# A decoder layer on one core: the tokens of every matrix product are divided at 320 of 576 instead of at 288

## The chip, the core and the metric

The kernel runs on one core of a Trainium2 chip. The time is the device time of one execution in microseconds, the median of three runs. The engines of the core are TensorE (PE in the profile; its weight loads are PEld), VectorE (DVE), ScalarE (ACT), GpSimd (POOL) and SyncE (SP), which issues the loads of weights.

## The reference

One inference step of one layer of a hybrid decoder, in fp32, on 512 prompt positions and 8 x 8 sampled positions, 576 tokens in all, with a model width of 2048.

```python
h = rmsnorm(x, norm_mix_g[l])
p = h @ w_in                                   # 2048 -> 5120: u_A, v_A, B_gate, C_gate, x_B
u = gelu(p[..., :o1]); v = rmsnorm(gelu(p[..., o1:o2]), sgu_norm_g)
y_a = u * chunk_sgu(v, w_s, b_s)               # 8 heads, chunks of 128 positions
zc, new_mix = causal_dwconv(cg * xb, mix_prev, conv_mix_w, conv_mix_b)
y = concatenate([group_rmsnorm(y_a, ...), group_rmsnorm(bg * zc, ...)])
x = x + y @ w_out                              # 2048 -> 2048
h = rmsnorm(x, norm_ffn_g)
gate, new_ffn = causal_dwconv(h @ w_gate, ffn_prev, conv_ffn_w, conv_ffn_b)   # 2048 -> 5632
x = x + (silu(gate) * (h @ w_up)) @ w_down     # 5632 -> 2048
```

The outputs are the final RMSNorm of both token groups, the last rows of the convolution inputs, and the normalised `v` rows of the sampled tokens.

## The kernel before

Everything is held transposed: features on the 128 partitions, the 576 tokens along the free dimension. `h_hi`, `h_lo` and `X` are 16 rows (`KT`) of 576 columns, one after the other in SBUF, each row 2304 bytes of a partition. Their place starts at `h_at`, the first place of the arena, which is rounded up to 32 bytes.

Each product in fp32 precision is made of three matmuls of fp32r operands, in the helper `three` (L1159 to L1163): high part of the weights with the high part of the activations, high with low, low with high. Each matmul loads 128 x 128 weights and streams the columns of one part of the tokens.

The 576 tokens don't fit one PSUM bank of 512 fp32 columns, so each output tile of 128 features has a pair of banks: `pair(p, half)` (L155) gives bank 2p + half, columns 0 to `HALF`, with `HALF` = 288 (L43). `gemm` (L1165) goes through the left half of the tokens with all 16 rows, in two slots of weights of 8 rows each (48 matmuls), and then through the right half with the same weights (48 matmuls). Each slot is given back by `piece_done` when the right half is through with it. `gemm2_by_k` (L1183) makes the first two tiles of `w_out` and of the feed-forward part row by row, left and right in turn by three matmuls, because the rows of its input are just being made. `down_tile` (L1365) adds a block of two rows of the activation (`act_hi`, `act_lo`) into one output tile of the down projection: six left matmuls, then six right.

The weights come as pieces of 128 x 1024: SyncE loads one into `raw` (two buffers), ScalarE rounds it to `w_hi` (`split_hi`, L485), VectorE makes `w_lo` from the rest (`split_lo`, L769). There are four slots of `w_hi` and `w_lo`. A product needs two, so while it runs on two, the other two are refilled; in the feed-forward loop (`ffn_block`, L1382) the sequence is gate tile, 16 down tiles of the block before, up tile, gate tile, up tile.

VectorE empties the banks: `times_rb` (L778) multiplies by the reciprocal norm, `w_out_tile` (L1021) and `down_add` (L1086) add to `X`, `gate_in` (L1058) writes the padded input of the convolution and so splits the right half into the rest of the prompt (224 columns) and the 64 sampled tokens. In each of them the left bank is read by one instruction and the right by the next, behind one wait for the whole tile. PSUM banks 4 to 7 serve small sums, transposes and the head mixing between the products; in the feed-forward loop they are two more pairs.

At the start, x comes in five blocks of tokens (four of 128, one of 64) and is transposed on TensorE. The first product may begin its left half when three blocks, 384 columns, are ready; `rest_of_x` (L1226) waits for the others before its right half.

Of the kernel before, what the change touches and what calls it, by code (L numbers as in the profile page):

```python
# [23 lines left out]
ALU = mybir.AluOpType  # L24
# [3 lines left out]
P = 128  # L28


def build_layer(nc, x_prompt, x_sample, state_conv_mix, state_conv_ffn, norm_mix_g, w_in, sgu_norm_g,
# [4 lines left out]
    _, SEQ, DM = x_prompt.shape  # L36
# [3 lines left out]
    assert w_s.shape[2] == P and AW % P == 0 and conv_mix_b.shape[1] == AW and DM == 2 * AW  # L40
    SAMP = NB * NS
    T = SEQ + SAMP
    HALF = T // 2  # L43
    KT = DM // P
    HEADS = AW // P
    TB = SEQ // P
# [12 lines left out]
    with ctx:  # L59
        def psum(name, shape):  # L60
            return ctx.enter_context(nc.psum_tensor(name, shape, F32))

        def sem(name):
            return ctx.enter_context(nc.semaphore(name))
# [7 lines left out]
        def sb(name, shape, dt=F32, at=None):  # L72
            n = 4
            for s in shape[1:]:
                n *= s
            n = -(-n // 32) * 32
            off = place[0] if at is None else at
            if at is None:
                place[0] += n
                assert place[0] <= base + ARENA, (name, place[0] - base)  # L80
            return nc.alloc_sbuf_tensor_at(name, shape, dt, offset=off)
# [4 lines left out]
        X = sb("X", [P, KT, T])  # L86
# [36 lines left out]
        rb = sb("rb", [P, T])  # L123
        zpad = sb("zpad", [P, ZP])
# [28 lines left out]
        ps = psum("ps", [P, 8, 512])  # L153

        def pair(p, half):  # L155
            return ps[:, 2 * p + half, 0:HALF]

        T_BANK, SSQ_BANK, MIX_BANK = 4, 5, 6
        t_samp = ps[0:SAMP, 7, 0:128]
# [9 lines left out]
        down_added = sem("down_added")  # L169
# [21 lines left out]
        tile_read = sem("tile_read")  # L191
# [51 lines left out]
        zs = zpad[:, 2 + SEQ:ZP].rearrange("p (b t) -> p b t", b=NB)  # L243

        def samp8(ap):

            return ap.rearrange("p (b t) -> p b t", b=NB)
# [13 lines left out]
        def blk_q(b):  # L261

            return b * 12 + (GEMM_PIECES - 4)

        def blk_p(b):

            return b * 8 + GEMM_PIECES
# [494 lines left out]
        def _(dve):  # L762

            v = nc.vector

            def row(buf, k):
                return buf[:, ds(k, 1), :].rearrange("p a t -> p (a t)")
# [9 lines left out]

            def times_rb(dst, p, done):  # L778

                v.tensor_tensor(dst[:, 0:HALF], pair(p, 0), rb[:, 0:HALF], ALU.mult)  # L780
                v.tensor_tensor(dst[:, HALF:T], pair(p, 1), rb[:, HALF:T], ALU.mult).then_inc(done, 1)  # L781

            def reciprocal_rms(n, dst):
                dve.wait_ge(rms_ready, n)
# [15 lines left out]
            for tb in range(TB + 1):  # L800
                n = P if tb < TB else SAMP
# [21 lines left out]
            for tb in range(TB + 1):  # L823
                n = P if tb < TB else SAMP
# [98 lines left out]
            with dve.Fori(1, HEADS // 2 - 1) as i:  # L923
                for s in range(2):
                    n = i * 2 + (s + 1)
# [95 lines left out]
            def w_out_tile(m, s, done=None):  # L1021

                dve.wait_ge(piece_done, m * 2 + (IN_PIECES + 2) if done is None else done)
                xm = row(X, m)
                v.tensor_tensor(xm[:, 0:HALF], xm[:, 0:HALF], pair(s, 0), ALU.add)
                v.tensor_tensor(xm[:, HALF:T], xm[:, HALF:T], pair(s, 1), ALU.add).then_inc(tile_read, 1)


            split_lo(IN_PIECES + 4, 0)
# [28 lines left out]
            def gate_in(f, p, done):  # L1058

                dve.wait_ge(piece_done, done)  # L1060
                dve.wait_ge(rows_saved, f + HEADS)
                n = SEQ - HALF
                v.tensor_tensor(zpad[:, 2:2 + HALF], pair(p, 0), rb[:, 0:HALF], ALU.mult)  # L1063
                v.tensor_tensor(zpad[:, 2 + HALF:2 + SEQ], ps[:, 2 * p + 1, 0:n], rb[:, HALF:SEQ], ALU.mult)
                v.tensor_tensor(zs[:, :, 2:], samp8(ps[:, 2 * p + 1, n:HALF]), samp8(rb[:, SEQ:T]),  # L1065
                                ALU.mult).then_inc(z_ready, 1)

            def gate_conv(f):
# [16 lines left out]

            def down_add(j, p, done):  # L1086
                dve.wait_ge(down_done, done)
                v.tensor_tensor(X[:, j, 0:HALF], X[:, j, 0:HALF], pair(p, 0), ALU.add)  # L1088
                v.tensor_tensor(X[:, j, HALF:T], X[:, j, HALF:T], pair(p, 1), ALU.add).then_inc(down_added, 1)  # L1089

            g0 = GEMM_PIECES
            split_lo(g0 + 4, 0)
            gate_in(0, 0, g0 + 3)
            split_lo(g0 + 5, 1)
            gate_conv(0)
# [7 lines left out]
            with dve.Fori(1, NBLK) as b:  # L1103
                q, p, d = blk_q(b), blk_p(b), (b - 1) * 16
# [44 lines left out]
            for tb in (0, 2, 4):  # L1149
                n = P if tb < TB else SAMP  # L1150
# [5 lines left out]
        def _(pe):  # L1156
# [8 lines left out]
            def gemm(q, c, p, q1=None, mid=None, q3=None):  # L1165


                for half in range(2):
                    cols = slice(half * HALF, (half + 1) * HALF)
                    for s in range(2):  # L1170
                        if half == 0:
                            pe.wait_ge(lo_ready, q + s + 1)
                        for k in range(PK):
                            kk = s * PK + k
                            last = three(pair(p, half), w_hi[:, (c + s) % 4, k, :], w_lo[:, (c + s) % 4, k, :],
                                         h_hi[:, kk, cols], h_lo[:, kk, cols], kk == 0, kk == KT - 1)
                        if half == 1:
                            last.then_inc(piece_done, 1)
                        hook = (q1, mid, q3, None)[2 * half + s]
                        if hook is not None:  # L1180
                            hook()

            def gemm2_by_k(q, ready, after):  # L1183


                for kk in range(KT):
                    s, k = kk // PK, kk % PK
                    pe.wait_ge(ready, kk + 1)
                    for tile in range(2):
                        c = 2 * tile + s  # L1190
                        if k == 0:
                            pe.wait_ge(lo_ready, q + c + 1)
                        for half in range(2):
                            cols = slice(half * HALF, (half + 1) * HALF)
                            last = three(pair(tile, half), w_hi[:, c, k, :], w_lo[:, c, k, :],
                                         h_hi[:, kk, cols], h_lo[:, kk, cols], kk == 0, kk == KT - 1)
                        if k == PK - 1:
                            last.then_inc(piece_done, 1)
                    if kk in after:
                        after[kk]()  # L1200
# [10 lines left out]
            for tb in range(TB + 1):  # L1211
                n = P if tb < TB else SAMP
# [39 lines left out]
                          start=True, stop=True).then_inc(corner_done, 1)  # L1252


            assert HALF <= 3 * P
            pe.wait_ge(xlo_pool, 2 * 3)
            pe.wait_ge(xlo_dve, 2 * 3)
            gemm(0, 0, 0, mid=rest_of_x)
# [106 lines left out]
            def down_tile(slot, jj, p, ks=(0, 1)):  # L1365

                for half in range(2):
                    cols = slice(half * HALF, (half + 1) * HALF)
                    for k in ks:
                        last = three(pair(p, half), w_hi[:, slot, 4 * k + jj, :], w_lo[:, slot, 4 * k + jj, :],  # L1370
                                     act_hi[:, k, cols], act_lo[:, k, cols], k == 0, k == 1)
                if ks[-1] == 1:
                    last.then_inc(down_done, 1)
# [88 lines left out]
            for tb in range(TB + 1):  # L1462
                n = P if tb < TB else SAMP
# [29 lines left out]
```

## Time and profile before

| | |
|---|---|
| median of 3 runs | 2510.88 us (2510.07 to 2511.1) |
| span of the profiled execution | 2507.9 us |
| mean granted clock of TensorE | 0.992 |
| matmuls in the span | 18473 |
| of these 128 x 128 by 288 columns | 18048 |
| loaded from memory | 208 MB, 87 GB/s with what is written |

The profile is of one execution. Its page gives busy times of each engine, the chain of work that ended last (followed back from the last instruction), and groups of instructions by line. The durations of matmuls on it overlap, since matmuls are pipelined and their ends are modelled; how often one starts after another is read from the timeline. The granted clock of TensorE is 1.0 (2.4 GHz) from about 60 us to the end of the products; before that it changes between the two levels.

### The profile page before, as it was taken

To read this page: it belongs to the slowest core of one execution; us is meant where nothing else is said; L and a number is where in the kernel's file an instruction comes from. 1 tells how busy PE (TensorE), PEld (TensorE's weight loads), DVE (VectorE), ACT (ScalarE), POOL (GpSimd) and SP (SyncE) were. 2 spreads that over 40 slices of the span, in tenths; PEclk is the share of its full clock that TensorE was granted. 3 is DMA by queue.
4 is the path that set the end of the run, shared out by engine and by line. 5 is a ranking of instruction groups with operands and counts; after the bars stand their busy time and mean duration, and the time that the engine had idled before them with its cause. 6 is when DMAs were issued, how large, how long until landed. Compare 5 with 4: busy or idle time off the path is not lost.

```text
span 2507.9 us, 45612 instructions
## 1 busy us (share of the span) xinstructions
PE 2462.1 (98%) x18473; PEld 2452.1 (98%) x18473; DVE 1206.8 (48%) x1902; ACT 617.1 (25%) x738; POOL 160.2 (6%) x279
## 2 busy tenths in 40 slices
PE   6999999999999999999999999999999999999996
PEld 6999999999999999999999999999999999999996
DVE  6357644556224535455434444444544354454445
ACT  6224312113113322222212222122222211222224
POOL 3310000001221000000000000000000000000004
PEclk8999999999999999999999999999999999999998
DMA  5422222224222222223222222222232222222222
GB/s 153 159 84 71 69 85 85 83 85 151 83 79 73 84 80 81 84 84 92 75 84 84 84 84 81 80 80 82 78 97 78 76 84 84 84 84 84 84 85 84
DMA packets 326837, 219.17 MB, mean 87 GB/s; under 512 B 6804, under 2 KB 301839, under 8 KB 324992
## 3 DMA queue, kind: packets, MB, share of 16 engines
q1 hardware_dynamic: 324432, 203.98, 27.2%
q0 software_dynamic: 2352, 14.41, 1.6%
q8 instruction: 41, 0.67, 0.1%
q14 instruction: 12, 0.10, 0.0%
HBM read 208.19 MB, written 10.18 MB: 87 GB/s over the span
## 4 chain that ended last, share of the span: by engine, by line
PE 96%; ACT 1%; DVE 1%; POOL 0%; issue 0%; DMA 0%; POOLq 0%; SPq 0%; DVEq 0%; ACTq 0%
PE ps L1161 32%; PE ps L1163 31%; PE ps L1162 31%; DVE h_lo L797 0%; POOL acc L470 0%; ACT ps L540 0%; PE ps L1284 0%; ACT h_hi L512 0%; PE ps L1297 0%; DMA x_nat<-in_x_prompt_dram 0%; ACT X L520 0%; PE ps L1296 0%; ACT w_hi L491 0%; DVE rms L813 0%; PE ps L1276 0%
## 5 line engine op out<-in xcount | busy, mean ns | idle before, releaser
L1161 PE MATMUL ps<-h_hi,w_hi 128*128 128x288 f32 x4608 | 1362.2, 296 | 6.2 <-issue 4.9
L1163 PE MATMUL ps<-h_hi,w_lo 128*128 128x288 f32 x4608 | 1358.7, 295 | 0.0
L1162 PE MATMUL ps<-h_lo,w_hi 128*128 128x288 f32 x4608 | 1358.3, 295 | 0.0
L1161 PEld LDWEIGHTS ps<-h_hi,w_hi 128*128 128x128 f32 x4608 | 865.6, 188 | 8.4 <-issue 5.8
L1162 PEld LDWEIGHTS ps<-h_lo,w_hi 128*128 128x128 f32 x4608 | 865.7, 188 | 0.0
L1163 PEld LDWEIGHTS ps<-h_hi,w_lo 128*128 128x128 f32 x4608 | 865.7, 188 | 0.0
L771 DVE TENSOR_TENSOR w_lo<-raw,w_hi 128x1024 fp32r<-128x1024 f32 x376 | 460.5, 1248 | 305.7 <-ACT w_hi L491 305.6
L491 ACT ACTIVATE w_hi<-raw 128x1024 fp32r<-128x1024 f32 x376 | 384.2, 1050 | 489.9 <-PE ps L1163 474.5
L1161 PE MATMUL ps<-act_hi,w_hi 128*128 128x288 f32 x1408 | 418.4, 297 | 1.0 <-DVE scaled L781 1.0
L1163 PE MATMUL ps<-act_hi,w_lo 128*128 128x288 f32 x1408 | 415.0, 295 | 0.0
L1162 PE MATMUL ps<-act_lo,w_hi 128*128 128x288 f32 x1408 | 414.3, 294 | 0.0
L1161 PEld LDWEIGHTS ps<-act_hi,w_hi 128*128 128x128 f32 x1408 | 264.4, 188 | 1.2 <-issue 1.2
L1163 PEld LDWEIGHTS ps<-act_hi,w_lo 128*128 128x128 f32 x1408 | 264.2, 188 | 0.0
L1162 PEld LDWEIGHTS ps<-act_lo,w_hi 128*128 128x128 f32 x1408 | 264.0, 187 | 0.0
L780 DVE TENSOR_TENSOR scaled<-ps,rb 128x288 f32<-128x288 f32 x68 | 31.1, 457 | 443.6 <-PE ps L1163 431.2
L1088 DVE TENSOR_TENSOR X<-X,ps 128x288 f32<-128x288 f32 x352 | 158.3, 450 | 81.4 <-PE ps L1163 81.4
L1063 DVE TENSOR_TENSOR zpad<-ps,rb 128x288 f32<-128x288 f32 x44 | 20.2, 458 | 305.8 <-PE ps L1163 305.8
L1089 DVE TENSOR_TENSOR X<-X,ps 128x288 f32<-128x288 f32 x352 | 157.3, 447 | 0.0
L620 ACT ACTIVATE cv<-zpad,ffnv 128x592 f32<-128x592 f32 x44 | 38.8, 882 | 417.8 <-DVE zpad L1065 417.8
L697 ACT ACTIVATE act_hi<-prod 128x576 fp32r<-128x576 f32 x44 | 30.2, 686 | 429.1 <-DVE prod L1080 429.1
L429 POOL COPY ffn_rows<-zpad 128x2 f32 x44 | 8.2, 187 | 1310.6 <-DVE zpad L1065 1310.6
L693 ACT ACTIVATE gate_act<-cv 128x592 f32<-128x592 f32 x44 | 30.8, 700 | 200.1 <-DVE cv L954 200.1
(184 smaller groups left out, 921.6 us busy)
## 6 DMA issues: line engine op xcount, KB each, us to landing
raw<-in_w_gate_dram SPq DMA_DIRECT2D x88, 512.0 KB, 3.9
raw<-in_w_up_dram SPq DMA_DIRECT2D x88, 512.0 KB, 3.8
raw<-in_w_down_dram SPq DMA_DIRECT2D x88, 512.0 KB, 4.3
raw<-in_w_in_dram SPq DMA_DIRECT2D x80, 512.0 KB, 4.3
raw<-in_w_out_dram SPq DMA_DIRECT2D x32, 512.0 KB, 4.0
xT_scratch<-X POOLq DMA_DIRECT2D x1, 4608.0 KB, 18.5
X<-xT_scratch POOLq DMA_DIRECT2D x4, 1152.0 KB, 5.6
x_nat<-in_x_prompt_dram SPq DMA_DIRECT2D x4, 1024.0 KB, 8.6
```

Of the source, the lines that this page charges most:

```text
L491: a.activation(w_hi[:, c % 4], raw[:, c % 2], ACT.Copy).then_inc(hi_ready, 1)
L620: a.activation(cv[:, :], zpad[:, 2:ZP], ACT.Identity, bias=b, scale=w).then_inc(tap2_done, 1)
L693: a.activation(gate_act[:, :], cv[:, :], ACT.Silu).then_inc(silu_done, 1)
L697: a.activation(act_hi[:, s, :], prod[:, :], ACT.Copy).then_inc(acthi_ready, 1)
L771: v.tensor_tensor(w_lo[:, c % 4], raw[:, c % 2], w_hi[:, c % 4].bitcast(F32), ALU.subtract).then_inc(lo_ready, 1)
L780: v.tensor_tensor(dst[:, 0:HALF], pair(p, 0), rb[:, 0:HALF], ALU.mult)
L1063: v.tensor_tensor(zpad[:, 2:2 + HALF], pair(p, 0), rb[:, 0:HALF], ALU.mult)
L1088: v.tensor_tensor(X[:, j, 0:HALF], X[:, j, 0:HALF], pair(p, 0), ALU.add)
L1089: v.tensor_tensor(X[:, j, HALF:T], X[:, j, HALF:T], pair(p, 1), ALU.add).then_inc(down_added, 1)
L1161: te.matmul(out, whi, xhi, start=start, stop=False)
L1162: te.matmul(out, whi, xlo, start=False, stop=False)
L1163: return te.matmul(out, wlo, xhi, start=False, stop=stop)
```

## The change

The left part of the tokens becomes five ninths, 320 columns, the right part 256. The two bounds stand in `CUTS`, and each place that used `HALF` uses them: the PSUM view `pair`, the columns that `gemm`, `gemm2_by_k` and `down_tile` stream, and VectorE's reads of the banks. The number of matmuls, weight loads, semaphores and waits is the same, and so is their order. In `gate_in` the right part's piece of the prompt is 192 columns instead of 224.

```diff
-    HALF = T // 2
+    LEFT = 5 * (T // 9)
+    CUTS = (0, LEFT, T)
...
         def pair(p, half):
-            return ps[:, 2 * p + half, 0:HALF]
+            return ps[:, 2 * p + half, 0:CUTS[half + 1] - CUTS[half]]
...
             def times_rb(dst, p, done):
 
-                v.tensor_tensor(dst[:, 0:HALF], pair(p, 0), rb[:, 0:HALF], ALU.mult)
-                v.tensor_tensor(dst[:, HALF:T], pair(p, 1), rb[:, HALF:T], ALU.mult).then_inc(done, 1)
+                v.tensor_tensor(dst[:, 0:LEFT], pair(p, 0), rb[:, 0:LEFT], ALU.mult)
+                v.tensor_tensor(dst[:, LEFT:T], pair(p, 1), rb[:, LEFT:T], ALU.mult).then_inc(done, 1)
...
-                n = SEQ - HALF
-                v.tensor_tensor(zpad[:, 2:2 + HALF], pair(p, 0), rb[:, 0:HALF], ALU.mult)
-                v.tensor_tensor(zpad[:, 2 + HALF:2 + SEQ], ps[:, 2 * p + 1, 0:n], rb[:, HALF:SEQ], ALU.mult)
-                v.tensor_tensor(zs[:, :, 2:], samp8(ps[:, 2 * p + 1, n:HALF]), samp8(rb[:, SEQ:T]),
+                n = SEQ - LEFT
+                v.tensor_tensor(zpad[:, 2:2 + LEFT], pair(p, 0), rb[:, 0:LEFT], ALU.mult)
+                v.tensor_tensor(zpad[:, 2 + LEFT:2 + SEQ], ps[:, 2 * p + 1, 0:n], rb[:, LEFT:SEQ], ALU.mult)
+                v.tensor_tensor(zs[:, :, 2:], samp8(ps[:, 2 * p + 1, n:T - LEFT]), samp8(rb[:, SEQ:T]),
                                 ALU.mult).then_inc(z_ready, 1)
...
-                v.tensor_tensor(X[:, j, 0:HALF], X[:, j, 0:HALF], pair(p, 0), ALU.add)
-                v.tensor_tensor(X[:, j, HALF:T], X[:, j, HALF:T], pair(p, 1), ALU.add).then_inc(down_added, 1)
+                v.tensor_tensor(X[:, j, 0:LEFT], X[:, j, 0:LEFT], pair(p, 0), ALU.add)
+                v.tensor_tensor(X[:, j, LEFT:T], X[:, j, LEFT:T], pair(p, 1), ALU.add).then_inc(down_added, 1)
...
                 for half in range(2):
-                    cols = slice(half * HALF, (half + 1) * HALF)
+                    cols = slice(CUTS[half], CUTS[half + 1])
```

The last edit is made in `gemm`, `gemm2_by_k` and `down_tile`, and the pair of adds also in `w_out_tile`.

## Rows read from the trace of the kernel before

**Rows 1.** Busy time of the engines over the span, from the page
```profile
PE 2462.1 (98%) x18473; PEld 2452.1 (98%) x18473; DVE 1206.8 (48%) x1902; ACT 617.1 (25%) x738; POOL 160.2 (6%) x279
```

**Rows 2.** Chain that ended last, shares of the span by engine and line
```profile
PE 96%; ACT 1%; DVE 1%; POOL 0%; issue 0%; DMA 0%; POOLq 0%; SPq 0%; DVEq 0%; ACTq 0%
PE ps L1161 32%; PE ps L1163 31%; PE ps L1162 31%; DVE h_lo L797 0%; POOL acc L470 0%; ACT ps L540 0%; PE ps L1284 0%; ACT h_hi L512 0%; PE ps L1297 0%; DMA x_nat<-in_x_prompt_dram 0%; ACT X L520 0%; PE ps L1296 0%; ACT w_hi L491 0%; DVE rms L813 0%; PE ps L1276 0%
```

**Rows 3.** TensorE's waits: us in total, times, longest; three of nine rows
```profile
PE ps L1219 <- ACT X L520: 7.7, 6, 3.3
...
PE ps L1161 <- issue: 4.9, 2, 2.9
...
PE ps L1161 <- DVE X L1026: 0.3, 1, 0.3
```

**Rows 4.** Groups of instructions: count | busy us, mean ns | idle before
```profile
L1161 PE MATMUL ps<-h_hi,w_hi 128*128 128x288 f32 x4608 | 1362.2, 296 | 6.2 <-issue 4.9
...
L1161 PE MATMUL ps<-act_hi,w_hi 128*128 128x288 f32 x1408 | 418.4, 297 | 1.0 <-DVE scaled L781 1.0
...
L1088 DVE TENSOR_TENSOR X<-X,ps 128x288 f32<-128x288 f32 x352 | 158.3, 450 | 81.4 <-PE ps L1163 81.4
```

**Rows 5.** A stretch: us, busy of PE, PEld, DVE, ACT, POOL; PEclk, DMA, GB/s
```profile
1000.00:1100.00 100.00, 100.00 (x756) 100.00 (x755) 50.02 (x89) 23.17 (x27) 1.62 (x9) 1.00 0.28 84
```

**Rows 6.** TensorE's timeline (start, duration): first left, first right, next tile
```profile
1048.49 0.29 PE L1161 MATMUL ps<-h_hi,w_hi 128*128 128x288 f32 x1
...
1054.81 0.30 PE L1161 MATMUL ps<-h_hi,w_hi 128*128 128x288 f32 x1
...
1061.21 0.29 PE L1161 MATMUL ps<-h_hi,w_hi 128*128 128x288 f32 x1
```

**Rows 7.** The same timeline, one down tile: first left, first right, next tile
```profile
1010.28 0.29 PE L1161 MATMUL ps<-act_hi,w_hi 128*128 128x288 f32 x1
...
1011.07 0.30 PE L1161 MATMUL ps<-act_hi,w_hi 128*128 128x288 f32 x1
...
1011.87 0.29 PE L1161 MATMUL ps<-act_hi,w_hi 128*128 128x288 f32 x1
```

**Rows 8.** TensorE's timeline, sums of 512 and 64 columns between products
```profile
179.32 0.40 PE L1296 MATMUL ps<-sq_hi,ones_r 128*128 128x512 f32 x1
...
179.79 0.19 PE L1296 MATMUL ps<-sq_hi,ones_r 128*128 128x64 f32 x1
179.82 0.27 PE L1297 MATMUL ps<-sq_lo,ones_r 128*128 128x64 f32 x1
179.93 0.38 PE L1161 MATMUL ps<-h_hi,w_hi 128*128 128x288 f32 x1
180.15 0.30 PE L1162 MATMUL ps<-h_lo,w_hi 128*128 128x288 f32 x1
```

**Rows 9.** TensorE's timeline in the first product, granted clock 0.50
```profile
38.32 0.44 PE L1162 MATMUL ps<-h_lo,w_hi 128*128 128x288 f32 x1
38.56 0.44 PE L1163 MATMUL ps<-h_hi,w_lo 128*128 128x288 f32 x1
```

**Rows 10.** TensorE's timeline, second slot of the products after `gemm2_by_k`
```profile
610.70 0.39 PE L1161 MATMUL ps<-h_hi,w_hi 128*128 128x288 f32 x1 [0.27 <-DVE X L1026]
...
822.00 0.29 PE L1163 MATMUL ps<-h_hi,w_lo 128*128 128x288 f32 x1
822.43 0.40 PE L1161 MATMUL ps<-h_hi,w_hi 128*128 128x288 f32 x1
```

**Rows 11.** Groups of instructions, as in rows 4: the splitting of the weights
```profile
L771 DVE TENSOR_TENSOR w_lo<-raw,w_hi 128x1024 fp32r<-128x1024 f32 x376 | 460.5, 1248 | 305.7 <-ACT w_hi L491 305.6
L491 ACT ACTIVATE w_hi<-raw 128x1024 fp32r<-128x1024 f32 x376 | 384.2, 1050 | 489.9 <-PE ps L1163 474.5
```

**Rows 12.** TensorE's timeline, four transposes and what follows them
```profile
160.90 0.60 PE L1276 MATMUL ps<-ident,vn 128*128 128x128 f32 x4
161.34 0.27 PE L1277 MATMUL ps<-ident,vn 128*64 128x128 f32 x1
```

More of the change, by code:

```diff
@@ L1024, in w_out_tile @@
                 xm = row(X, m)
-                v.tensor_tensor(xm[:, 0:HALF], xm[:, 0:HALF], pair(s, 0), ALU.add)
-                v.tensor_tensor(xm[:, HALF:T], xm[:, HALF:T], pair(s, 1), ALU.add).then_inc(tile_read, 1)
+                v.tensor_tensor(xm[:, 0:LEFT], xm[:, 0:LEFT], pair(s, 0), ALU.add)
+                v.tensor_tensor(xm[:, LEFT:T], xm[:, LEFT:T], pair(s, 1), ALU.add).then_inc(tile_read, 1)
             split_lo(IN_PIECES + 4, 0)
@@ L1193, in gemm2_by_k @@
                         for half in range(2):
-                            cols = slice(half * HALF, (half + 1) * HALF)
+                            cols = slice(CUTS[half], CUTS[half + 1])
                             last = three(pair(tile, half), w_hi[:, c, k, :], w_lo[:, c, k, :],
@@ L1252, in corner @@
                           start=True, stop=True).then_inc(corner_done, 1)
-            assert HALF <= 3 * P
+            assert LEFT <= 3 * P
             pe.wait_ge(xlo_pool, 2 * 3)
@@ L1367, in down_tile @@
                 for half in range(2):
-                    cols = slice(half * HALF, (half + 1) * HALF)
+                    cols = slice(CUTS[half], CUTS[half + 1])
                     for k in ks:
```

## The prediction

> **What bounds the kernel now.** I read the page's busy table first: TensorE is busy 98% of the span in matmuls and weight loads alike, VectorE 48%, ScalarE 25% [rows 1]. A busy TensorE could still be an engine waiting inside modelled durations, so I went to the chain that ended last: 96% of it is TensorE, and three lines of the helper `three` carry 94% [rows 2]. The third view is the list of what TensorE waited for: nine rows, from 7.7 down to 0.3 us, 27 us in all, nearly all of it ahead of the first product and between stages [rows 3]. So the time is a count times a period: 3 x 4608 products on `h` and 3 x 1408 on `act`, 18048 in all, each 288 columns wide [rows 4]. The mean duration printed there (295 ns) overlaps its neighbours and is no period. The period comes from the stretches: 756 matmuls in 100 us at full clock, 132.3 ns each [rows 5]. 18048 x 132.5 = 2391 us of the 2507.9 us span; the rest is the start, the end, the transposes and small sums. What matters is therefore the period at 320 and at 256 columns, and nothing else by much: 1 ns on the mean of the two is 18 us, 0.7% of the time. The measurement of this kernel can tell about 0.2%, that is 5 us or 0.28 ns per matmul.
>
> **What the trace says of the period.** In one undisturbed product of a tile, the 48 matmuls of the left half go from 1048.49 to 1054.81 (6.32 us, 131.7 ns each) and the 48 of the right half from there to 1061.21 (6.40 us, 133.3 ns each) [rows 6]. The down products show the same order: six left ones 0.79 us, six right ones 0.80 us [rows 7]. So the two halves of equal width differ by 1.6 ns, and I don't know the cause. The one other width of the same operand type is 512: two matmuls of 512 columns follow each other and the next starts 0.47 us after the first, 235 ns each (the 16 such pairs lie within 4 ns of that) [rows 8]. The line through (288, 132.5) and (512, 235) has a slope of 102.5 / 224 = 0.458 ns per column and passes zero columns at +0.7 ns: time is proportional to columns, 2.18 columns per ns, with hardly a fixed part. At 1.2 GHz the same 288 columns take 0.24 us, 1.2 columns per ns and no more [rows 9].
>
> **The change part by part.**
> (1) The 9024 left matmuls grow from 288 to 320 columns: +32 x 0.458 = +14.7 ns, 147.2 ns. The 9024 right ones shrink to 256: -14.7 ns, 117.8 ns. Sum per pair: 265.0 ns as before, so +132.3 us and -132.3 us, net 0. This holds for every straight line, with or without a fixed part; no matmul, weight load, semaphore or wait is added. Only a departure from the line inside 256 to 320 counts, and the trace has no row there. I bound it from both sides below, under the rivals, and take 0 because both measured widths lie on a line through nearly nothing.
> (2) A wait: `gemm` starts its second slot of weights 24 left matmuls after the first. After each of the two products by rows (`gemm2_by_k`), the slot was freed late and the matmul that needs it starts late: with 0.27 us of idle time before it at 610.70, and 0.43 us after its predecessor at 822.43, where 0.13 us is the rule, so 0.30 us late [rows 10]. The 24 left matmuls ahead of it now last 24 x 14.7 = 0.35 us longer, while the slot's refill (one ScalarE copy, one VectorE subtraction) begins at the same moment. Both waits, 0.27 and 0.30 us, are covered by that: -0.6 us. What is late next is nothing: the right half behind is shorter by the same 0.35 us.
> (3) Slots in the steady part are given back after the first half of the right pass, which now ends 9.88 us instead of 9.52 us into a product of 12.7 us: 0.35 us later. ScalarE and then VectorE refill it from `raw`, in 1.05 and 1.25 us [rows 11]; the slot is wanted a whole product later, 12.7 us. The cost is nothing; if that cover were gone it would be at most 0.35 us a tile, for which a wait of every tile on VectorE's `w_lo` would have to stand in the wait list, and none does [rows 3].
> (4) VectorE reads both banks after the right part is done. The add to `X` of one bank takes 450 ns [rows 4]. If all of that were by the column, 1.6 ns each, the left read grows by 0.05 us and the right shrinks by as much; the prompt's piece in `gate_in` goes from 224 to 192 and the left grows by the same 32. Sum 0, and it lies beside TensorE, except at the ends of stages, where the sum is equal too.
> (5) The first product starts at 1.2 GHz [rows 9], and the clock rises within its left half. The left half waits for three blocks of x, as before, since 320 columns are still within 384; the wait for the rest of x shows no idle time, and comes later now. 0 us.
> (6) At the end, `down_tile` of the last block is paced partly by GpSimd's sums. They start from the VectorE add, whose sum is equal. 0 us.
> Sum: 2507.9 - 0.6 = 2507.3 us for the profiled execution. The median of the runs is 2510.9, 3.0 us above the span; so 2510.3.
>
> At one place a rule of the Trainium skill bears on this. The page "TensorE: Matmul & The Clock Gate", section "Back-to-back issue gap", gives N / 2.4 + 2.5 ns: an estimate from it is 122.5 ns for 288 columns, where this trace has 132.5; so its slope (0.417) is too small here. By its formula 135.8 and 109.2 ns would have the same mean as two of 122.5, so the sum would still be 0.
>
> **The rivals.**
> (A) The period depends on where the read starts. Rows of `h_hi` are 576 x 4 = 2304 bytes, nine times 256. The cut at 288 puts the right half 1152 bytes in, 4.5 times 256; at 320 it is 1280, five times 256, in step with the left half. If the 1.6 ns by which right exceeds left [rows 6, 7] comes from that half step, the right part becomes as cheap as the left: 9024 x 1.6 = 14.4 us less, 2495.8 us. For: the difference is there in two kinds of product, with equal width, equal weights and the same rows. Against: left and right also go to different banks of PSUM, and that doesn't change; and the left read could as well be the odd one.
> (B), the slower side: the read goes in blocks of 256 bytes, and each block touched costs something. Today both halves lie in step at one end and half a block off at the other, five blocks each. Whether the buffer itself starts on a block can't be seen. If it is half a block off, 320 columns touch six and 256 touch five: eleven for ten. The price: 288 columns at 2.4 GHz are 120 ns, so 12.5 ns of the 132.5 are over; divided by five blocks, 2.5 ns each. One more block for each pair is 9024 x 2.5 = +22.6 us, 2532.8 us. It decides only if the buffer starts off a block. If it starts on one, the blocks would be 5 + 4, nine for ten, and the same price would be a gain to 2487.6. Against both: 512 columns are 21.7 ns over their 213.3, which a straight line explains as well.
> (C) The weight load becomes the bound of the right part. Each matmul loads 128 columns of weights, and in one stretch the trace shows that this has a price: after two matmuls of 64 columns (179.79) the starts are 0.03, 0.11 and 0.22 us apart, 0.36 us for three, although the streams would be 0.03, 0.03 and 0.13 [rows 8]. Taken as three loads in a row that is at most 120 ns a load, against 117.8 ns for a right matmul; taken with the last one as a 288-column stream of 132 ns, it is 114 ns. The transposes of 128 columns, each with its load, are 0.44 us for four, 110 ns [rows 12]. So the floor is 110 to 120 ns: below the 117.8 it costs nothing, at 120 it costs 2.2 x 9024 = 19.9 us, 2530.1. The transposes are the plainest row of a load per matmul; I take no cost, and keep the other end.
> The Trainium skill's same page, section "LDWEIGHTS (loading the stationary operand)", gives columns / 1.2 ns; an estimate from it is 106.7 ns for this load, under the 117.8, and the transposes' 110 ns agrees with it.
> (D) The change doesn't do what it says: the program would have to split differently from the text. The shapes are static, so I give this nothing.
>
> **How the numbers follow.** Straight line, within 5 us of 2510.3: 0.42. Start of the read (A) and blocks from an aligned buffer, 2488 to 2500: 0.28. Blocks from an unaligned buffer (B), 2525 to 2535: 0.18. Weight load or the like (C), 2516 to 2530: 0.12. Predicted is the straight line's 2510.3; its own range is 2505 to 2515. The range over the cases reaches down to A with a little over, 2494, and up past B's price, 2534; it leaves out the block gain and larger losses, together under 0.2. Faster by over 0.2%: 0.28; within 0.2%: 0.42; slower by over 0.2%: 0.30.
>
> **What the profile after would show.** (1) right and the line holding: 48 left matmuls of a product in 7.07 us, 48 right in 5.65 us, and again 756 in 100 us. If A: the left at 146.3 ns or so and the right at 117 ns, both on one line. If B: both above the line by one block's 2.5 ns in part. If C: the left on the line and the right above 118 ns, whatever the left does. (2) right: the gaps at the two places near 0.13 us. (3) and (4): the wait list as short as before. The prediction is wrong if the sum of one left and one right period departs from 265 ns by more than 0.6 ns; the other terms together can't move 1 us.

## The result, and the profile after

The changed kernel takes 2524.1 us (2522.4 to 2525.3) where the kernel before took 2511.0 in the same comparison: 1.0049 times as long, with an interval of 1.0034 to 1.0063. The forecast of no change was wrong: it is 0.5% slower, by about 13 us, inside the stated range but clear of zero. The profiled span went from 2507.9 to 2521.4 us.

The page's busy table, in the columns of [rows 1], and the chain, in those of [rows 2]:

```profile
PE 2475.4 (98%) x18473; PEld 2465.8 (98%) x18473; DVE 1206.4 (48%) x1902; ACT 617.1 (24%) x738; POOL 160.5 (6%) x279
PE 96%; ACT 1%; DVE 1%; POOL 0%; issue 0%; DMA 0%; POOLq 0%; SPq 0%; DVEq 0%; ACTq 0%
```

The same picture and the same counts: TensorE alone carries the end, VectorE did the same work in the same time. TensorE's waits show nothing new either (us in total, times, longest; the first three of nine rows, for [rows 3]; lines after L43 are one further on in this kernel):

```profile
PE ps L1220 <- ACT X L521: 7.9, 6, 3.5
PE ps L1220 <- DMA x_nat<-in_x_prompt_dram: 6.3, 2, 3.3
PE ps L1162 <- issue: 4.9, 2, 2.9
```

So the time came from the period. TensorE's timeline (start, duration) in the feed-forward part shows the first right matmul of a tile, the first left one of the next, its first right one and the first left one after it; the last three answer to [rows 6]:

```profile
1048.32 0.28 PE L1162 MATMUL ps<-h_hi,w_hi 128*128 128x256 f32 x1
...
1054.08 0.31 PE L1162 MATMUL ps<-h_hi,w_hi 128*128 128x320 f32 x1
...
1061.12 0.28 PE L1162 MATMUL ps<-h_hi,w_hi 128*128 128x256 f32 x1
...
1066.88 0.31 PE L1162 MATMUL ps<-h_hi,w_hi 128*128 128x320 f32 x1
```

48 left matmuls take 7.04 us, 146.7 ns each; 48 right ones 5.76 us, 120.0 ns each. The pair is 266.7 ns; it was 131.7 + 133.3 = 265.0 ns. Over all tiles, by the median tile: in the 13440 matmuls of `gemm` the period rose from 132.5 to 133.3 ns, 0.81 ns each, 10.9 us; in the 4224 of the down products from 132.75 to 133.33, 2.5 us; in the 384 of `gemm2_by_k` it was 133.3 and stayed. That is 13.4 us of the 13.5 by which the span grew.

From here on it helps to count in array cycles at 2.4 GHz, 0.4167 ns each, and to take the width off: the left half before took 316 cycles (288 + 28), the right 320 (288 + 32); after the change they take 352 (320 + 32) and 288 (256 + 32). The widths add to 576 in every case. What moved is the surcharge, the cycles above the width: 60 a pair became 64, and the four are all the left half's, 28 before and 32 after; the right half pays 32 at either width.

### The profile page after: what moved, and what is told of

It reads as the page before. It is cut to its first block, busy times and chain, and to the rows that moved or that the text cites. A ratio compares the mean times of both kernels' runs of the same rounds, so it can differ in the third digit from the quotient of the medians.

```text
span 2521.4 us, 45612 instructions
## 1 busy us (share of the span) xinstructions
PE 2475.4 (98%) x18473; PEld 2465.8 (98%) x18473; DVE 1206.4 (48%) x1902; ACT 617.1 (24%) x738; POOL 160.5 (6%) x279
## 4 chain that ended last, share of the span: by engine, by line
PE 96%; ACT 1%; DVE 1%; POOL 0%; issue 0%; DMA 0%; POOLq 0%; SPq 0%; DVEq 0%; ACTq 0%
PE ps L1162 32%; PE ps L1164 31%; PE ps L1163 31%; DVE h_lo L798 0%; POOL acc L471 0%; ACT ps L541 0%; PE ps L1285 0%; ACT h_hi L513 0%; PE ps L1298 0%; ACT X L521 0%; DMA x_nat<-in_x_prompt_dram 0%; PE ps L1297 0%; PE ps L1277 0%; DVE rms L814 0%; PE ps L1446 0%
## 5 line engine op out<-in xcount | busy, mean ns | idle before, releaser
L1162 PE MATMUL ps<-h_hi,w_hi 128*128 128x256 f32 (+1 forms) x4608 | 1369.5, 297 | 6.0 <-issue 4.9
L1163 PE MATMUL ps<-h_lo,w_hi 128*128 128x256 f32 (+1 forms) x4608 | 1365.6, 296 | 0.0
L1164 PE MATMUL ps<-h_hi,w_lo 128*128 128x256 f32 (+1 forms) x4608 | 1365.5, 296 | 0.0
L1162 PE MATMUL ps<-act_hi,w_hi 128*128 128x256 f32 (+1 forms) x1408 | 418.0, 297 | 1.0 <-DVE scaled L782 1.0
L1164 PE MATMUL ps<-act_hi,w_lo 128*128 128x256 f32 (+1 forms) x1408 | 416.7, 296 | 0.0
L1163 PE MATMUL ps<-act_lo,w_hi 128*128 128x256 f32 (+1 forms) x1408 | 416.7, 296 | 0.0
L781 DVE TENSOR_TENSOR scaled<-ps,rb 128x320 f32<-128x320 f32 x68 | 33.3, 490 | 445.9 <-PE ps L1164 433.4
L1089 DVE TENSOR_TENSOR X<-X,ps 128x320 f32<-128x320 f32 x352 | 169.6, 482 | 83.9 <-PE ps L1164 83.9
L1064 DVE TENSOR_TENSOR zpad<-ps,rb 128x320 f32<-128x320 f32 x44 | 21.7, 492 | 310.3 <-PE ps L1164 310.3
L1090 DVE TENSOR_TENSOR X<-X,ps 128x256 f32<-128x256 f32 x352 | 145.1, 412 | 0.0
```

The costliest lines, as they stand in the source:

```text
L781: v.tensor_tensor(dst[:, 0:LEFT], pair(p, 0), rb[:, 0:LEFT], ALU.mult)
L1064: v.tensor_tensor(zpad[:, 2:2 + LEFT], pair(p, 0), rb[:, 0:LEFT], ALU.mult)
L1089: v.tensor_tensor(X[:, j, 0:LEFT], X[:, j, 0:LEFT], pair(p, 0), ALU.add)
L1090: v.tensor_tensor(X[:, j, LEFT:T], X[:, j, LEFT:T], pair(p, 1), ALU.add).then_inc(down_added, 1)
L1162: te.matmul(out, whi, xhi, start=start, stop=False)
L1163: te.matmul(out, whi, xlo, start=False, stop=False)
```

## The experiments

The kernels that are timed differ from the changed kernel, or in one case from the kernel before, by the one to three lines shown. Each stream kernel is the kernel before with matmuls behind its last one whose results nothing reads; its time as a whole means nothing. A stream is a row of 32 to 96 equal matmuls, and the granted clock is 1.0 in all streams quoted but those of 96 to 160 columns in the last section.

### Widths on their own, three theories

```diff
             last.then_inc(fssq_done, 1)
+            mv = act_hi[:, :, :].rearrange("p k t -> p (k t)")
+            def probe(i, n, a, bank, m=P, src=mv, same=False):
+                return (ps[0:m, bank, 0:n], w_hi[:, 0, 0 if same else i % PK, 0:m], src[:, a:a + n])
+            for i in range(64): te.matmul(*probe(i, 256, 0, 2), start=i == 0, stop=i == 63)
...
```

> The kernel before, and behind its last matmul 57 short streams of fp32r matmuls (64 or 96 each, 128 columns of weights, eight weight blocks in turn) that nothing reads: widths 64 to 512 from the first column of act_hi, then 288 columns from eleven other starts, two banks, weights of 64 and 32 columns, one weight block again and again, and high, low, high in turn. In the changed kernel 320 columns take 146.7 ns and 256 take 120.0 ns, that is each width plus 32 array cycles of 2.4 GHz. Theory 1, a fixed cost of 32 cycles a matmul, which only 288 columns in the left half escape: 256 columns 120.0 ns, 272 columns 126.7, 304 columns 140.0, 240 columns 113.3, each 16 columns 6.7 ns. Theory 2, a floor near 120 ns from the weight load (rival C) over a line of 0.458 ns per column: 224, 240 and 256 columns all about 120 ns, 272 columns about 125 and 304 about 140; 64 weight columns lower the floor, so that 256 columns then take about 117.8 ns or less. Theory 3, the start of the read (rivals A and B): 288 columns change with the start in steps of 64 or 256 bytes, by 1.6 ns or more, and 256 columns take less at one of the starts 0, 32, 64 and 320 than at the others.

The view is that of one source line: count, duration (min/median/max), first and last start in us, shape. The period is the distance of the two starts by 63:

```profile
L1481 PE MATMUL ps<-act_hi,w_hi x64: 269/274/280, 2578.5 to 2585.5; 128*128 128x240 f32 x64
L1483 PE MATMUL ps<-act_hi,w_hi x64: 278/283/283, 2592.9 to 2600.4; 128*128 128x256 f32 x64
L1485 PE MATMUL ps<-act_hi,w_hi x64: 284/288/291, 2608.2 to 2616.1; 128*128 128x272 f32 x64
L1487 PE MATMUL ps<-act_hi,w_hi x64: 290/295/298, 2624.4 to 2632.7; 128*128 128x288 f32 x64
L1489 PE MATMUL ps<-act_hi,w_hi x64: 296/301/303, 2641.5 to 2650.2; 128*128 128x304 f32 x64
L1491 PE MATMUL ps<-act_hi,w_hi x64: 308/309/313, 2659.5 to 2668.7; 128*128 128x320 f32 x64
L1501 PE MATMUL ps<-act_hi,w_hi x64: 294/294/297, 2770.7 to 2779.1; 128*128 128x288 f32 x64
L1512 PE MATMUL ps<-act_hi,w_hi x64: 274/281/287, 2864.0 to 2871.4; 128*128 128x256 f32 x64
L1521 PE MATMUL ps<-act_hi,w_hi x64: 274/276/280, 2936.0 to 2943.1; 128*64 128x256 f32 x64
```

From the single starts, which are kept in ns, the means past the first few are:

| columns (from column 0) | 208 to 240 | 248 | 256 | 264 | 272 | 280 | 288 | 296 | 304 | 312 | 320 | 352 | 384 | 448 | 512 |
|---|---|---|---|---|---|---|---|---|---|---|---|---|---|---|---|
| ns | 111.6 | 113.3 | 120.0 | 120.0 | 125.4 | 127.9 | 131.8 | 136.0 | 137.7 | 142.7 | 146.7 | 160.0 | 173.3 | 206.7 | 227.1 |
| cycles above the width | (floor) | 24 | 32 | 24 | 29 | 27 | 28 | 30 | 27 | 31 | 32 | 32 | 32 | 48 | 33 |

The streams give the periods of the kernels to 0.1 ns (131.7 for the old left, 146.7 and 120.0 for the new halves), although no other engine and no DMA works beside them. Neither contention nor the schedule has a part in it. From 248 to 384 columns the surcharge is no line: it goes up and down between 24 and 32 cycles, and beyond them it has 48 at 448 columns and 33 at 512. 288 columns from column 32 (L1501) take 133.3 ns, as from column 288, where the old right half began; from 0, 64, 128, 192 and 256 they take 131.7, and from 144 as well. The bank makes no difference (131.8 in bank 3). Nor does the turn of `act_hi` and `act_lo`, or one weight block again and again (131.6 each). Theory 1 falls with 264 and 304 columns. Theory 2 falls with 224 and 240, which were to take about 120 ns as 256 do: a floor exists, and it lies at 111.6 ns, where 208, 224 and 240 columns are alike, 8 ns under what 256 columns take. Weights have a part all the same: with 64 weight columns (L1521) the same 256 columns take 113.5 ns, 16 cycles above the width instead of 32. But 320 columns stay at 146.7 with them, and 512 take 230.0, more than the 227.1 with 128. Theory 3 is right for 288 columns, and for 256 too: they are at +32 from 0, 64 and 320, but take 118.6 ns from 32 (L1512). Only 320 columns don't depend on the start here, at +32 from 0, 32, 64 and 256.

### The change mirrored

```diff
-    LEFT = 5 * (T // 9)
+    LEFT = 4 * (T // 9)
```

> The changed kernel mirrored: left part 256 columns, right part 320. Theory 1 (fixed cost by width) and theory 2 (floor under 256 columns): left 120.0 ns, right 146.7 ns, the time as after the change, 2524 us, but for the two waits for a slot of weights behind the products by rows, which grow by 0.35 us each. Theory 3 (the start of the read or the bank of the left half is what was cheap at 288 columns): the time differs from 2524 us by more than 3 us.

2524.9 us (2523.8 to 2526.5), 1.0050 with an interval of 1.0033 to 1.0067. The periods changed sides, as theories 1 and 2 had it: 120.0 left, 146.7 right. Side and bank have no part in the loss.

### Half of the change

```diff
-    LEFT = 5 * (T // 9)
+    LEFT = 304
```

> Half of the change: the cut at 304, a left part of 304 columns and a right part of 272. Theory 1 (width plus 32 cycles for every width but the equal halves): 140.0 and 126.7 ns, 133.3 in the mean, the time as after the change, 2523 us. Theory 2 (a floor near 120 ns that 272 columns stay above, on a line of 0.458 ns per column): 139.7 and 125.2 ns, 132.5 in the mean, the time as before, 2510 us. Theory 3: right part starts 1216 bytes in, 4.75 times 256, so it is as dear as at 288 or dearer, 2511 us or more.

2480.6 us (2477.7 to 2481.5), 0.9874 with an interval of 0.9858 to 0.9891: 1.3% faster than before, which no theory had. TensorE's timeline, first left, first right, next tile:

```profile
1050.73 0.30 PE L1162 MATMUL ps<-h_hi,w_hi 128*128 128x304 f32 x1
...
1057.34 0.29 PE L1162 MATMUL ps<-h_hi,w_hi 128*128 128x272 f32 x1
...
1063.26 0.30 PE L1162 MATMUL ps<-h_hi,w_hi 128*128 128x304 f32 x1
```

6.61 us and 5.92 us, 137.7 and 123.3 ns: surcharges of 27 and 24 cycles, 51 a pair instead of 60. 272 columns from column 0 had 125.4 ns as a stream, from column 304 they have 123.3. So going half the way gains and going the whole way loses; a slope between two widths cannot say what a third one costs.

### Every buffer 128 bytes further on

```diff
-        place = [base]
+        place = [base + 128]
```

> The kernel before with 288 and 288 columns, every buffer in SBUF 128 bytes further on, the distances between them as they were. Theory 3 (where the read starts against blocks of 256 bytes decides, rivals A and B): left and right change roles, 133.3 ns for the left and 131.7 for the right. Theories 1 and 2: nothing changes, 131.7 and 133.3 ns, and the time stays at 2511 us.

2511.8 us, 1.0002 with an interval of 0.9993 to 1.0012, and 131.6 to 131.7 left and 133.4 right in the products, as before. Left and right did not change roles, so the start of the read against fixed places of 256 bytes (rival A as it stood) is out. Rival B is not tested by this: 1152 bytes touch five blocks by its count whether the buffer is shifted or not. What matters for 288 columns is not where they lie in SBUF but where they lie against something that moved with them.

### All cuts, and starts and weights moved

```diff
+            def probe(i, n, a, off=0, m=P):
+                return (ps[0:m, 2, 0:n], wv[:, off + (i % PK) * P:off + (i % PK) * P + m], mv[:, a:a + n])
...
+            for i in range(48): te.matmul(*probe(i, 256, 0, 16), start=i == 0, stop=i == 47)
...
```

> The kernel before, and behind its last matmul 111 streams of 48 fp32r matmuls that nothing reads: for 34 cuts c from 248 to 328 the left part (c columns from column 0) and the right part (576 - c columns from column c); then 256, 320, 304 and 272 columns from starts 8 to 56 columns on; then the weight blocks 16, 32 and 64 columns off; then 32, 64 and 96 columns of weights. The streams measured so far: 288 from 0 131.7 ns, 288 from 288 133.3, 320 from 0 146.7, 256 from 320 119.9, 304 from 0 137.7, 272 from 0 125.4, 264 from 0 120.0. Theory 4: the moving columns and the weight columns of the next matmul are read against each other, and what a matmul pays above its width (24 to 32 array cycles) hangs on width and start in steps of 8 to 16 columns, with its worst where the width is a multiple of 32 and the start a multiple of 64. Then 272 columns from 304 take about 123.3 ns as in the kernel with that cut; 256 and 320 columns become cheaper at some starts that are no multiple of 32; 32 and 64 weight columns make 256 and 304 columns cheaper than 128 do, 96 lie between. Theory 5: the cost above the width hangs on the width alone. Then no start and no place of the weights changes a stream by over 0.5 ns, and 272 columns from 304 take 125.4 ns, which the kernel with that cut already speaks against. The best pair by theory 4 lies among the cuts 296 to 312; by a line through 288 and 512 columns no pair is better than another.

The same view, the period now the distance by 47: 256 columns from column 0, from column 16, from 0 with the weights 16 columns on, from 0 with 32 weight columns, and 320 columns with 32:

```profile
L1479 PE MATMUL ps<-act_hi,w_hi x48: 281/283/283, 2532.2 to 2537.9; 128*128 128x256 f32 x48
L1544 PE MATMUL ps<-act_hi,w_hi x48: 276/276/279, 2944.6 to 2950.0; 128*128 128x256 f32 x48
L1566 PE MATMUL ps<-act_hi,w_hi x48: 276/276/280, 3084.6 to 3089.9; 128*128 128x256 f32 x48
L1575 PE MATMUL ps<-act_hi,w_hi x48: 276/276/277, 3141.7 to 3147.1; 128*32 128x256 f32 x48
L1577 PE MATMUL ps<-act_hi,w_hi x48: 304/304/308, 3153.8 to 3160.6; 128*32 128x320 f32 x48
```

5.7 us against 5.4: 256 columns cost 120.0 ns from column 0 and 113.3 from column 16, and 113.3 as well when the weights are moved instead. With 32 or 64 weight columns they cost 113.3, with 96 116.0. For 288 columns, moving the start alone by 32 columns (the first streams) or the weights alone by 32 (here) turns 131.7 ns into 133.3, and moving both (the experiment before) changes nothing. This takes rival B's blocks away: moving the weights alone by 16 leaves the blocks of the moving columns as they were, and yet takes 6.7 ns off. 320 columns stay at 146.7 ns at all eight starts and three places of the weights, and only 32 weight columns lower them, to 143.3. Of the pairs, the cut 276 was the best with 621.7 cycles, then 304 (626.8), 260 (627.5) and 248 (628.4); 288 had 635.9, 320 and 256 had 640.0, 262 655.1. Theory 5 is out. Theory 4 has the dependence on the start and on the weights right, with 272 columns from 304 at 123.3 ns as it said, and three of its forecasts missed: 320 columns became cheaper at no start, 304 columns were not cheaper with fewer weight columns (138.4 ns with 32, 137.8 with 64, 140.0 with 96, 137.8 with 128), and the best cut lay at 276 and not between 296 and 312. It says what the price hangs on, not why.

### The best cut of the streams, in the kernel

```diff
-    LEFT = 5 * (T // 9)
+    LEFT = 276
```

> The changed kernel with the cut at 276: a left part of 276 columns and a right part of 300. Theory 4 (width and start decide, by what the streams of their own took: 125.6 ns for 276 from 0 and 133.3 ns for 300 from 276, 129.5 in the mean against 132.5 of the kernel before): 18048 x 3.0 = 54 us less than the kernel before, 2457 us. A straight line, or width plus 32 cycles: 2511 or 2524 us.

2484.6 us (2482.9 to 2485.7), 0.9890 with an interval of 0.9873 to 0.9906: half of the 54 us. TensorE's timeline, first left, first right, next tile:

```profile
1050.68 0.29 PE L1162 MATMUL ps<-h_hi,w_hi 128*128 128x276 f32 x1
...
1056.84 0.30 PE L1162 MATMUL ps<-h_hi,w_hi 128*128 128x300 f32 x1
...
1063.26 0.29 PE L1162 MATMUL ps<-h_hi,w_hi 128*128 128x276 f32 x1
```

The right matmuls take 133.7 ns, as the stream's 133.3; the left ones 128.3, where the stream had 125.6. 9024 x 2.7 = 24 us is what is missing.

### The change with the weights moved

```diff
     LEFT = 5 * (T // 9)
...
+        place[0] += 64
         w_at = place[0]
...
+        place[0] += 192
         q_at = place[0]
```

> The changed kernel, 320 and 256 columns, and nothing else but w_hi and w_lo 64 bytes (16 columns) further on in SBUF; what lies behind them is 256 bytes further on. Theory 4 (moving columns and weight columns are read against each other): the right part goes from 120.0 to 113.3 ns, the left part stays at 146.7, the mean goes from 133.3 to 130.0 ns, so 18048 x 3.3 = 60 us less than after the change, 2464 us, below the kernel before too. Theory 1 or 5 (the width alone decides) and theory 2 (a floor from the weight load): 120.0 ns and 2524 us, since neither width nor load changes.

2480.4 us (2477.1 to 2501.6), 0.9896 with an interval of 0.9848 to 0.9944; three of the four executions took 2477.1 to 2481.1, and the one of 2501.6 left no trace. With the cut of the change untouched, 64 bytes between two buffers take 44 us off its time, and put it 1% under the kernel before. Width, load and every instruction are those of the changed kernel, so neither the width alone nor a floor can be the cause of its loss. Two tiles of this kernel, one of the `w_out` products and one of the feed-forward part, first right matmul and next tile:

```profile
651.46 0.28 PE L1164 MATMUL ps<-h_hi,w_hi 128*128 128x256 f32 x1
...
657.11 0.31 PE L1164 MATMUL ps<-h_hi,w_hi 128*128 128x320 f32 x1
...
1060.11 0.28 PE L1164 MATMUL ps<-h_hi,w_hi 128*128 128x256 f32 x1
...
1065.56 0.30 PE L1164 MATMUL ps<-h_hi,w_hi 128*128 128x320 f32 x1
```

5.65 us and 5.45 us for 48 matmuls: 117.7 ns in one stage and 113.5 in the other, for the same width, the same columns of the same buffers and the same places of weights. This is why less than 60 us came: the `w_out` stage, a part of the first product, and the down products with 116.5 ns on the right, sit on a dearer step.

### Twelve places of the weights

Streams as before, for ten cuts with the weights 0 to 56 columns off.

> The kernel before, and behind its last matmul 242 streams of 32 fp32r matmuls that nothing reads: ten cuts with the weights 0 to 56 columns off, twelve places. Theory 4: the cost above the width changes with the place of the weights, and some pair of cut and place is below the 621.7 cycles (129.5 ns a matmul) of the cut 276 at place 0; shifting both the weights and the start by 16 columns gives the cost of neither shifted. Theory 5: all places give the row of place 0.

The place changes every cut, each in a way of its own: 276 has between 621 and 644 cycles, 304 between 626 and 642, 288 between 631 and 640. The expectation had some pair clearly below the 621.7 of 276 at place 0, and none was: 276 itself has 621.0 here, and 316 with 48 is level with it at 621.5. With the weights at 16, 256 columns from column 0 had 27 cycles above the width here (117.8 ns) and 16 in the stream of all cuts (113.3).

The other half of the expectation, that shifting both gives the cost of neither shifted, can be read from the right halves whose start is as far beyond a multiple of 64 as the weights are moved. From the single starts of this run, of the streams of all cuts and of the next experiment, in ns (two values where the turns differ):

| columns, moved by | neither moved | start alone | weights alone | both |
|---|---|---|---|---|
| 288, by 32 | 131.7 | 133.3 | 133.3 | 131.7 to 131.9 |
| 272, by 48 | 125.4, 126.6 | 123.3 | 126.7 | 125.2 to 125.4 |
| 296, by 24 | 136.0 | 137.0 | 136.7 | 135.9 |
| 300, by 20 | 136.7, 139.9 | 133.3 | (no row) | 136.7 |

Two rows of this run show it for 300 columns from column 276, weights unmoved and moved by 20; the period is the distance by 31:

```profile
L1482 PE MATMUL ps<-act_hi,w_hi x32: 296/296/302, 2533.4 to 2537.6; 128*128 128x300 f32 x32
L1582 PE MATMUL ps<-act_hi,w_hi x32: 297/298/303, 2956.9 to 2961.2; 128*128 128x300 f32 x32
```

4.2 and 4.3 us. With both moved, 304 columns by 16, 280 by 40, 264 by 56 and 312 by 8 also come within 0.2 ns of a value that they have with neither moved; 316 by 4 alone is off, with 144.0 against 143.4. So what decides is where the moving columns lie against the weight columns, and not where either lies by itself.

### What ran before

```diff
+            def probe(i, n, a, off=0):
+                k = i // 3 % PK
+                return (ps[:, 2, 0:n], wv[i % 3][:, off + k * P:off + k * P + P], av[i % 3][:, a:a + n])
...
+            for i in range(24): te.matmul(*probe(i, 288, 0, 16), start=i == 0, stop=i == 23)
+            for i in range(48): te.matmul(*probe(i, 256, 0, 16), start=i == 0, stop=i == 47)
+            for i in range(24): te.matmul(*probe(i, 320, 0, 16), start=i == 0, stop=i == 23)
+            for i in range(48): te.matmul(*probe(i, 256, 0, 16), start=i == 0, stop=i == 47)
...
```

> The kernel before, and behind its last matmul streams that nothing reads, now in the order of gemm: 48 left matmuls (high, low, high in turn, weights from w_hi, w_hi, w_lo), then 48 right ones, the pair twice over, for 13 cuts and six places of the weights; then the same stream behind five different ones. The kernel with the cut at 276 had 128.3 ns for its left matmuls where the stream of its own had 125.6, and 256 columns from 320 with weights 16 columns on had 113.6 ns in the kernel and about 118 in a stream of its own. Theory 6 (the two reads fall into one of several steps with each other, and which one hangs on what ran before): the first and the second pair of a cut differ in some rows by over 1 ns, and 276 columns or 256 columns behind five different streams take at least two values. Theory 7 (the turn of high, low and w_lo is what changes 276 columns, since other buffers are read): first and second pair agree within 0.5 ns, 276 from 0 takes 128.3 ns behind every stream. By both, 288/288, 304/272 and 320/256 with unshifted weights take 132.5, 130.6 and 133.3 ns in the mean as in the kernels.

256 columns from column 0 with the weights 16 columns on, once behind 24 matmuls of 288 columns (L1799), once behind 24 of 320 (L1801); each row is every third matmul, 15 x 3 = 45 periods from its first start to its last:

```profile
L1799 PE MATMUL ps<-act_hi,w_hi x16: 276/276/279, 4534.8 to 4539.9; 128*128 128x256 f32 x16
...
L1801 PE MATMUL ps<-act_hi,w_hi x16: 280/281/281, 4543.8 to 4549.1; 128*128 128x256 f32 x16
```

5.1 and 5.3 us: 113.3 ns behind 288, 264 or 512 columns, 117.8 behind 320 or 300, and it stays there for all 48. The same 256 columns from column 320 take 113.3 behind 264 and 512 only, and 117.8 behind 288 too. 276 columns from 0 take 125.6 behind 288, 264 and 512 and 126.7 behind 320 and 300. Of the 156 halves 12 differ by more than 1 ns between the first and the second turn of their pair. One of them is 276 from 0 with unmoved weights: 25 cycles above the width in its first turn, 32 in its second, behind the 48 right matmuls of its own pair, and 276 + 32 cycles are 128.3 ns, the kernel's value. Behind 24 of the same right matmuls it took 126.7, so the width just ahead doesn't settle it alone. 288/288, 304/272 and 320/256 gave 636, 627 and 640 cycles both times. So theory 6 is what the runs show, and theory 7 is out.

### A pair that held in both turns

```diff
-    LEFT = 5 * (T // 9)
+    LEFT = 260
...
+        place[0] += 32
         w_at = place[0]
...
+        place[0] += 224
         q_at = place[0]
```

> The changed kernel with the cut at 260 (left 260, right 316 columns) and w_hi and w_lo 32 bytes (8 columns) further on: the best pair that held in both turns of the streams, 624 cycles of 2.4 GHz for the two, 130.0 ns in the mean. Theory 6 (width, start, place of the weights, and what ran before, in steps): the gate and up products show 120.0 ns left (260 + 28 cycles) and 140.0 ns right (316 + 20), the time is 18048 x 2.5 = 45 us under the kernel before, 2466 us; as the kernels with the cut 276 and with shifted weights showed, down products and products by rows can settle on a dearer step, so up to 20 us of it may be missing. A straight line, or the width alone: 2505 to 2511 us.

2472.9 us (2471.4 to 2473.7), 0.9846 with an interval of 0.9829 to 0.9862, the fastest of the study, 1.5% under the kernel before and 2% under the changed one. The products take 120.0 and 140.1 ns, as forecast from the streams (120.0 and 140.0); the down products 120.3 and 140.8. 7 us of the 45 are missing.

## Why the prediction was wrong

**The bound and the count were right.** The time is 18048 periods, no wait appeared, and 13.4 of the 13.5 us are in the period. The rule stated with it, that the prediction is wrong if the pair departs from 265 ns by over 0.6, was the one that fired: 266.7.

**Term (1) failed: the straight line.** It put 147.2 and 117.8 ns on the new halves, net 0; they take 146.7 and 120.0. The left term was 0.5 ns too high, 4.5 us; the right one 2.2 ns too low, 20 us. The difference, 15 us, is 13.4 in the span, since the pair of the down products and of `gemm2_by_k` stood at 265.5 and 266.7 ns already before. A line through two widths can't be checked by two widths. Its end at 512 [rows 8] was read from pairs of matmuls at 235 ns each, while a stream of 512 columns takes 227.1: a pair between other matmuls is no measure of the period in a stream. With 227.1 the slope is 0.42 ns per column, close to one array cycle, so the prediction was wrong to call a slope of 0.417 too small. That alone would have left the sum at 0, as any line does; what a line can't hold is a surcharge that is 28 cycles for the old left half and 32 for the other three. And the one sign in the trace that the line was no law, two equal widths 1.6 ns apart [rows 6], was kept as a rival when it was the finding: it meant that the surcharge of 28 to 32 cycles depends on more than the width, and that half a percent of the time lay in it.

**Rival A** named the start of the read. It is right that the start matters for 288 columns (131.7 from multiples of 64 columns, 133.3 from 32 beyond one), though against the weights and not against fixed places. It is wrong that 320 columns in step would make the new right half cheap: at width 256 with these places the price is 32 cycles from each start that is a multiple of 64. **Rival B** had the right sign and a mechanism that the weights moved alone speak against. **Rival C** had the time within its bounds and its signs in the profile after, the left half on the line and the right above 118 ns, but by luck: it had the size for the right half (2.2 ns), and its floor exists, but at 111.6 ns; the 120.0 is not a floor, since 256 columns go down to 113.3 when they or the weights are moved by 16 columns.

**Term (2)** was half right. The late matmul at 822.43 [rows 10] is gone in the trace after, a gain of 0.3 us. The other, at 610.70, is there as before, and its row after shows why:

```profile
612.66 0.28 PE L1164 MATMUL ps<-h_hi,w_lo 128*128 128x256 f32 x1
613.21 0.41 PE L1162 MATMUL ps<-h_hi,w_hi 128*128 128x320 f32 x1 [0.27 <-DVE X L1027]
```

It stands between a right half and the next left half: it waits for VectorE's read of the pair of banks, not for a slot of weights in the middle of a left half, as I took it.

**Terms (3) to (6)** held: no wait on `w_lo`, VectorE at 1206.4 us busy where it had 1206.8, the waits at the start and the end as before to 0.3 us.

What is shown: the price of a matmul above its width changes with the width, with where the moving columns lie against the weight columns, with how many weight columns are loaded, and with what ran before; it is the same without any other engine at work. That the place counts only as one against the other is shown by the rows with both moved and by the kernel with every buffer moved. That the read of the next weights and the read of the moving columns disturb each other is the reading that fits all of these, but it was only argued. Which buffer or port they share, and why the steps are what they are, stays open.

## What to carry to other kernels

Where a kernel is bound by a steady stream of fp32r matmuls, measure the period of each width at its start and place of weights instead of drawing a line between widths; some five thousand spare matmuls behind the last one gave a hundred of them in one run, and in the products of the cuts 288, 304 and 320 kernel and stream agreed to 0.1 ns. Equal halves are no optimum by themselves: cuts 16 columns apart differed by 1.7%, and 64 bytes between two buffers were worth as much. Confirm the choice in the kernel, since what ran before can put it on a dearer step.

## What the runs showed of the hardware

Streams of 96, 128 and 160 columns took 213.3 ns each while the granted clock was 0.50, and 208, 224 and 240 columns 111.6 ns each at 1.00, with 128 weight columns in each: a floor that follows the clock (1.9 times) and not the width. It hangs on the weights: with 64 or 32 weight columns 128 columns took 60.0 ns at 1.00, far under it. The view by stretches (us; busy of PE, PEld, DVE, ACT, POOL; granted clock, DMA, GB/s) for the stream of 160 and for that of 240 columns:

```profile
2541.00:2554.00 13.00, 13.00 (x63) 13.00 (x62) 0.00 (x0) 0.00 (x0) 0.00 (x0) 0.50 0.00 0
2579.00:2585.00 6.00, 6.00 (x56) 6.00 (x55) 0.00 (x0) 0.00 (x0) 0.00 (x0) 1.00 0.00 0
```

At 1.2 GHz the 288 columns of the first product had no surcharge at all, 0.24 us [rows 9], 16 times in a row in the single starts: for this width it is there only at 2.4 GHz. And in the streams a step, once taken, was kept: 48 matmuls of 256 columns in a row stayed at 113.3 or at 117.8 ns, by what had run ahead of them.
